# Prompt attention of a streaming encoder layer: the next pair's projection moved to steps 2 to 21, its norms across the edge, and a new slot table

## The chip, the cores and the metric

One core of a Trainium2 chip runs the whole layer in one launch. The metric is the device time of a run in microseconds; the median of three runs is compared.

## The reference, cut to what matters

The layer normalizes its input, projects it once (`w_in`), runs a recurrent branch and an attention branch, merges them and adds a mixture of experts. The change touches the attention branch alone, for a prompt of 1024 positions and for 64 new positions of a running stream with a cache of 2048:

```python
z = xn @ w_in
u_x, u_g, q, k, v, f_logit, g_rnn, g_attn = jnp.split(z, SPLIT_POINTS, axis=-1)
q = _rmsnorm(q.reshape(B, T, N_HEADS, HEAD_DIM), q_norm_g)
k = _rmsnorm(k.reshape(B, T, N_HEADS, HEAD_DIM), k_norm_g)
...
s = jnp.einsum('bqhd,bkhd->bhqk', q_blk, k).astype(jnp.float32) * scale
s = s + cq_blk.astype(jnp.float32).transpose(0, 2, 1)[..., None] - ckT
s = jnp.where(k_pos[None, :] <= q_pos[:, None], s, NEG_INF)
p = jax.nn.softmax(s, axis=-1)
return jnp.einsum('bhqk,bkhd->bqhd', p.astype(v.dtype), v)
```

There are 16 heads of 64. The normed k and the v are outputs too, for the prompt and for the stream.

## The kernel before

`attend` goes over 8 pairs of heads. The pairs 0 to 5 are turns of a loop, the pairs 6 and 7 are written out behind it. Pair i's attention is done in 24 steps, and while it runs, the q, k and v of pair i+1 are projected, normed and turned (`ahead`). Each engine runs its own program over the same steps; they meet in semaphores. Between pair i's step 23 and pair i+1's step 0 lies the edge of a pair.

**The steps.** `STEPS` lists four units (two heads, two halves of the queries) with their key tiles: unit 0 has steps 0 to 3, unit 1 steps 4 to 7, unit 2 steps 8 to 15, unit 3 steps 16 to 23. TensorE's program of a step s is: `score(s+1)` (L1125, L1127, and L1130 on the diagonal), then part 0 (a projection quarter, then the items of the slot), then `weigh(s)` (L1145), which needs ScalarE's `exp(s)` (L1344), then part 1 (a quarter, items). The tiles of scores and of probabilities have two buffers each.

**The projection.** A pair's 9 tiles of 128 positions have four quarters each, so 36 quarters, and a quarter is six products (`product`, L101 to L103) of 384 columns. Before, they go in pairs in the steps 0 to 17 (`PROJECT_STEPS`). There is one bank for them, `proj_ps`: behind the fourth quarter ScalarE copies it out and squares (`take_tile`), VectorE sums the squares (`sum_squares`), and only then may the next tile follow the copy. With tiles 0 to 3 done `mean 0` may run on VectorE, with tiles 4 to 8 `mean 1`; then ScalarE's `root` (L1295, a square root, behind which a small exponential L1385 brings the exponential's table back), then VectorE's `norm` 0 to 3 (L1463, L1464; tiles 0-1, 2-3, 4-5, 6-8), each of which raises `kv_ready`.

**The weights.** The projection's weights are in two parts, high and low. For pair i+2 they can be made only when pair i+1's projection has ended: SyncE loads w_in (L258) into one of two raw buffers, ScalarE rounds (`round_w`, L1289, items w 0 to 2), GpSimd subtracts (`rest_w`, L965). The columns of q (0) and v (2) share a raw buffer, so that the load of 2 waits for GpSimd's `rest_w` of 0, and `w 2` on ScalarE waits for that load.

**The items.** `SLOTS` says by hand which further work lies in which step and part. On each engine they are in the order of the table, and an engine waits where it stands:

- `max n`: a chunk of scores on TensorE (L1068, L1071) for the rows' maxima, one bank, reduced by VectorE (L1485). max 0 to 3 are for the next pair's unit 0, 4 to 7 for unit 1, and so on. `rows u` turns the maxima (L1059), ScalarE copies them (L1305), and `score` of the unit's first step waits for that.
- `qk0 b`, `qk1 b`: a head's q and k turned (L1053), copied by ScalarE (L1300, L1301) and by VectorE (`take_cross`, L1474). b is a batch of two tiles; b 0 and 1 are of the next pair, b 2 and 3 of this one. They wait for `kv_ready` of norm b.
- The stream: `qs`, `past n` (cached keys turned), `ss n` (scores of chunk n, L1204, L1205), their maximum (L1555) and exponential (L1378), `sp n` (turned, L1217, copied L1391), `sw n` (weighed, L1230, copied L1563). Chunk 4 is the short tail. Then `sum` (VectorE, L1569 to L1575) and `o` (turned, L1241). All items that turn share two banks, `turn_ps`, in strict alternation.
- `out u`: VectorE divides a unit's output (L1526, L1527). `out 3` comes behind step 23.

GpSimd also copies v (`take_v`), a part of the keys (`copy_high`, L972), and issues `load_c` (rows of the cumulated gates, L942; max 4 of the next pair waits for head 1's, `c_loaded`), `load_past_v` and `load_c_stream`. SyncE's queue holds the loads of weights and cached keys, the stores of k and v (L894 to L898) and of the attention's output (L907).

Of the kernel before, what the change touches and what calls it, by code (L numbers as in the profile page):

```python
# [775 lines left out]
def attend(nc, g):  # L776
# [10 lines left out]
    PROJECT_STEPS = 18  # L787
# [20 lines left out]
    FIRST_MAXES = 4  # L808
    NO_TURN = ("max", "out", "mean", "root", "norm", "w", "sum")
    later = lambda item: item[0] in ("mean", "root", "norm", "w") or item == ("rows", 0) or \  # L810
# [15 lines left out]
    with ExitStack() as ctx:  # L826
# [21 lines left out]
        warm = sb("warm", [P, 1])  # L848
# [15 lines left out]
        kv_ready, kv_stored, vs_copied = sem("kv_ready"), sem("kv_stored"), sem("vs_copied")  # L864
# [17 lines left out]
        with nc.Block() as block:  # L882
            @block.sync
            def _(sp):
# [7 lines left out]
                def store_kv(p):  # L892
                    sp.wait_ge(kv_ready, p * BATCHES + BATCHES)
                    sp.dma_start(heads(g.out_k_p[0, 0], p), qk_sb[:, 0:PT, 2:4, :].rearrange("p t h d -> p t (h d)")).then_inc(kv_stored, 16)  # L894
                    sp.dma_start(heads(g.out_v_p[0, 0], p), v_next[:, 0:PT, :]).then_inc(kv_stored, 16)
                    stream = lambda ap: ap.rearrange("t h d -> t (h d)")[:, bass.ds(p * P, P)]
                    sp.dma_start(stream(g.out_k_s[0, 0]), qk_sb[0:T_SAMPLE, PT, 2:4, :].rearrange("p h d -> p (h d)")).then_inc(kv_stored, 16)
                    sp.dma_start(stream(g.out_v_s[0, 0]), v_next[0:T_SAMPLE, PT, :]).then_inc(kv_stored, 16)  # L898
# [15 lines left out]
                store_kv(0)  # L914
                for done in g.early:
                    sp.sem_clear(done)
                with sp.Fori(0, PAIRS - 2) as i:
                    sp.wait_ge(w_split, i * 3 + 6)
                    alone(sp, g)
                    load_w(sp, g, i + 2, 0)  # L920
                    load_w(sp, g, i + 2, 1)
                    sp.wait_ge(w_split, i * 3 + 7)
                    alone(sp, g)
                    load_w(sp, g, i + 2, 2)
                    store_kv(i + 1)
                    probs_turned(i)
# [1392 lines left out]
```

## Time and profile before

| | |
|---|---|
| three runs | 2758.89, 2759.14, 2765.78 us; median 2759.14 |
| the profiled execution | 2751.23 us, of which the instructions span 2749.7 us |
| mean granted TensorE clock | 0.916 |
| TensorE, products | 2257.4 us busy (82%) |
| VectorE | 1328.1 us (48%) |
| ScalarE | 1116.7 us (41%) |
| GpSimd | 223.6 us (8%) |
| attention's pairs | from 185 to 1142 us |

Times in the trace are microseconds from the start of the span. "Idle before" is the time that an engine had nothing running ahead of an instruction, with what ended it. A granted clock of 1 is TensorE at 2.4 GHz, one of 0.5 at 1.2 GHz.

### The profile page before, as it was taken

To read this page: it belongs to the slowest core of one execution; us is meant where nothing else is said; L and a number is where in the kernel's file an instruction comes from. 1 tells how busy PE (TensorE), PEld (TensorE's weight loads), DVE (VectorE), ACT (ScalarE), POOL (GpSimd) and SP (SyncE) were. 2 spreads that over 40 slices of the span, in tenths; PEclk is the share of its full clock that TensorE was granted. 3 is DMA by queue.
4 is the path that set the end of the run, shared out by engine and by line. 5 is a ranking of instruction groups with operands and counts; after the bars stand their busy time and mean duration, and the time that the engine had idled before them with its cause. 6 is when DMAs were issued, how large, how long until landed. Compare 5 with 4: busy or idle time off the path is not lost. (4 is left out here: it accounts for less than half of the span.)

```text
span 2749.7 us, 36614 instructions
## 1 busy us (share of the span) xinstructions
PE 2257.4 (82%) x11080; PEld 1748.6 (64%) x11080; DVE 1328.1 (48%) x1548; ACT 1116.7 (41%) x1520; POOL 223.6 (8%) x294
## 2 busy tenths in 40 slices
PE   4459797887979797699899959989917999999991
PEld 2447565665757574499887849975415766666660
DVE  4334444445354444421155542111136888777884
ACT  3223343433333343221155632101105777777770
POOL 0210201202020200000012100000020000000002
PEclk9779898988989897899999979999958999999995
DMA  2210202112020202221156542133036999999986
GB/s 84 64 40 1 79 0 79 29 50 56 24 79 0 63 0 56 77 66 38 51 155 186 185 133 68 46 118 125 0 130 250 387 374 369 366 362 366 377 317 236
DMA packets 207115, 377.28 MB, mean 137 GB/s; under 512 B 20508, under 2 KB 128200, under 8 KB 206968
## 3 DMA queue, kind: packets, MB, share of 16 engines
q1 hardware_dynamic: 184680, 302.07, 32.2%
q0 software_dynamic: 18784, 61.92, 7.1%
q10 hardware_dynamic: 3584, 12.58, 1.2%
q8 instruction: 20, 0.33, 0.0%
q14 instruction: 47, 0.39, 0.0%
HBM read 301.87 MB, written 74.66 MB: 137 GB/s over the span
## 5 line engine op out<-in xcount | busy, mean ns | idle before, releaser
L2132 DVE TENSOR_TENSOR e_w_lo<-e_raw,e_w_hi 128x2048 fp32r<-128x2048 f32 x192 | 438.3, 2290 | 116.1 <-ACT e_w_hi L2059 107.2
L2059 ACT CAST e_w_hi<-e_raw 128x2048 fp32r<-128x2048 f32 x192 | 366.6, 1911 | 142.9 <-DMA e_raw<-w_down_e 60.0
L101 PE MATMUL proj_ps<-w_qkv_hi,xh 128*128 128x384 f32 x544 | 233.0, 428 | 21.6 <-PEq L286 19.2
L1145 PE MATMUL out_ps<-mT 128*128 128x512 f32 (+3 forms) x384 | 181.0, 556 | 23.2 <-ACT mT L1344 18.3
L103 PE MATMUL proj_ps<-w_qkv_hi,xl 128*128 128x384 f32 x544 | 187.9, 345 | 0.0
L102 PE MATMUL proj_ps<-w_qkv_lo,xh 128*128 128x384 f32 x544 | 187.3, 344 | 0.0
L1485 DVE TENSOR_REDUCE neg_part<-max_ps 128x1 f32<-128x512 f32 (+3 forms) x128 | 75.4, 589 | 133.0 <-PE max_ps L1071 72.7
L1344 ACT ACTIVATE mT<-st_ps 128x512 f32<-128x512 f32 x192 | 93.3, 489 | 109.1 <-PE st_ps L1130 48.3
L1671 PE MATMUL m_prod<-m_w_o,mT 128*128 128x512 f32 (+1 forms) x288 | 127.5, 602 | 11.2 <-DMA m_w_o<-w_o 11.2
L101 PEld LDWEIGHTS proj_ps<-w_qkv_hi,xh 128*128 128x128 f32 x544 | 107.2, 197 | 46.2 <-issue 40.7
L101 PE MATMUL e_gate_ps<-e_w_hi,e_xT_hi 128*96 128x512 f32 x256 | 105.8, 413 | 21.2 <-issue 10.5
L1474 DVE TENSOR_TENSOR qk_cross<-turn_ps,qk_high 64x256 fp32r<-64x256 f32 x128 | 53.4, 417 | 143.1 <-ACT qk_cross L1301 136.2
L102 PEld LDWEIGHTS proj_ps<-w_qkv_lo,xh 128*128 128x128 f32 x544 | 106.4, 196 | 20.6 <-issue 15.4
L1068 PE MATMUL max_ps<-qk_high 66*128 66x512 f32 (+1 forms) x192 | 82.0, 427 | 44.8 <-DVE extra L1485 33.4
L1125 PE MATMUL st_ps<-qk_high 67*128 67x512 f32 x192 | 89.5, 466 | 29.5 <-ACT qk_high L1305 18.0
L101 PE MATMUL e_y_ps<-e_w_hi,e_hT_hi 128*96 128x512 f32 x256 | 103.9, 406 | 11.1 <-DVE e_hT_lo L2140 9.1
L1526 DVE RECIPROCAL out_T<-out_ps 64x512 f32<-64x512 f32 x32 | 107.3, 3353 | 6.9 <-DVE o_part L1563 2.4
L1448 DVE TENSOR_REDUCE qk_rstd<-qk_squares 128x4 f32<-128x256 f32 x72 | 30.2, 420 | 160.3 <-ACT qk_squares L1284 157.9
L101 PE MATMUL e_up_ps<-e_w_hi,e_xT_hi 128*96 128x512 f32 x256 | 102.7, 401 | 4.1 <-issue 2.7
L103 PEld LDWEIGHTS proj_ps<-w_qkv_hi,xl 128*128 128x128 f32 x544 | 105.4, 194 | 0.0
L1671 PEld LDWEIGHTS m_prod<-m_w_o,mT 128*128 128x128 f32 (+1 forms) x288 | 53.4, 188 | 79.7 <-issue 68.2
L103 PE MATMUL e_gate_ps<-e_w_hi,e_xT_lo 128*96 128x512 f32 x256 | 102.8, 402 | 0.0
(402 smaller groups left out, 5330.3 us busy)
## 6 DMA issues: line engine op xcount, KB each, us to landing
e_raw<-w_gate_e SPq DMA_DIRECT2D x64, 1024.0 KB, 13.8
e_raw<-w_up_e SPq DMA_DIRECT2D x64, 1024.0 KB, 14.1
e_raw<-w_down_e SPq DMA_DIRECT2D x64, 1024.0 KB, 13.0
slot_x<-zrows POOLq DMA_DIRECT2D x48, 440.0 KB, 6.4
e_x<-slot_x SPq DMA_DIRECT2D x33, 384.0 KB, 11.3
w_raw<-w_in SPq DMA_DIRECT2D x24, 512.0 KB, 4.5
slot_y<-e_y ACTq DMA_DIRECT2D x32, 384.0 KB, 6.2
slot_y<-zrows POOLq DMA_DIRECT2D x24, 352.0 KB, 9.6
```

The lines of the kernel that those rows point to most:

```text
L101: nc.tensor.matmul(out, a_hi, b_hi, start=start, stop=False)
L102: nc.tensor.matmul(out, a_hi, b_lo, start=False, stop=False)
L103: return nc.tensor.matmul(out, a_lo, b_hi, start=False, stop=stop)
L1068: last = te.matmul(max_ps[:, 0:w], high[0:HD + 2, h, 0, t * P:(t + 1) * P], high[0:HD + 2, h, 1, c0:c0 + w], start=True, stop=not diagonal)
L1125: te.matmul(out[:, 0:q1 - q0], high[0:HD + 3, h, 1, j * P:(j + 1) * P], high[0:HD + 3, h, 0, q0:q1], start=True, stop=False)
L1145: te.matmul(out_ps[u % 2][:, q0 - c * BANK:BANK], v_one[:, j, h, :], probsT[s % 2][:, 0:q1 - q0], start=(j == 0), stop=(s == last_step(u)) ...
L1344: sc.activation(probsT[s % 2][:, 0:q1 - q0], st_ps[s % 2][:, 0:q1 - q0], ACT.Exp).then_inc(exp_ready, 1)
L1485: v.tensor_reduce(out, max_ps[:, 0:w], X_AXIS, ALU.max, negate=True).then_inc(max_taken, 1)
L1526: chain(v.reciprocal(into, out_ps[u % 2][other, n0:n1]))
L1671: last = te.matmul(prod[0:rows(t), t % 2, c * BANK:(c + 1) * BANK], g.mT[:, k, t * P:t * P + rows(t)], w_o[:, k, c * BANK:(c + 1) * BANK], ...
L2059: sc.copy(w_hi[u][:, :], w.raw[c][:, :]).then_inc(wh_ready, 1)
L2132: v.tensor_tensor(w_lo[u][:, :], w.raw[c][:, :], w_hi[u][:, :], ALU.subtract).then_inc(wl_ready, 1)
```

## The change

The quarters of the projection lie in the steps 2 to 17 in pairs and in the steps 18 to 21 one by one (36 as before). Norm 3 of a pair is done in step 1 of its own attention, norm 2 behind `o` in step 23; mean 1 goes to step 21, root 1 to 22, w 0 to 2 to 22 and 23, sum to 21. The stream's chunks have other slots: ss 0 in 5 instead of 7, ss 3 in 12 instead of 16, ss 4 in 14 instead of 18. qk0 3 goes from step 1 to step 2, behind rows 1. The stores of k and v go in two halves of 4 tiles. SyncE loads the cached keys ahead of the third weight load. GpSimd has another order. ScalarE begins each pair with a small exponential of its own.

```diff
-    PROJECT_STEPS = 18
+    PROJECT = {s: (1, 1) if s < 18 else (0, 1) for s in range(2, 22)}
+    LAST_NORM = 3
+    KV_STORES = (2, 4)
-    SLOTS = {0: ((), (("qk0", 2), ("max", 4))), 1: ((("max", 5),), (("qk0", 3), ("max", 6))),
-             2: ((("max", 7),), (("rows", 1), ("max", 8))), 3: ((("max", 9),), (("qs", 0), ("max", 10))),
-             4: ((("max", 11),), (("past", 0), ("max", 12))), 5: ((("max", 13),), (("past", 1), ("max", 14))),
-             6: ((("max", 15),), (("rows", 2), ("out", 0))), 7: ((("qk1", 2),), (("ss", 0), ("mean", 0))),
-             8: ((("qk1", 3),), (("sp", 0), ("max", 16))), 9: ((("max", 17), ("root", 0)), (("ss", 1),)),
-             10: ((("max", 18), ("sw", 0)), (("sp", 1),)), 11: ((("max", 19), ("past", 2)), (("sw", 1), ("norm", 0))),
-             12: ((("max", 20),), (("ss", 2), ("max", 21))),
-             13: ((("max", 22), ("sp", 2)), (("past", 3), ("max", 23), ("norm", 1))),
-             14: ((("rows", 3),), (("sw", 2), ("out", 1))), 15: ((), (("out", 2),)),
-             16: ((("qk0", 0),), (("ss", 3),)), 17: ((("qk0", 1),), (("sp", 3), ("mean", 1))),
-             18: ((("max", 0), ("w", 0)), (("sw", 3), ("ss", 4), ("root", 1))),
-             19: ((("max", 1), ("norm", 2)), (("sp", 4), ("w", 1))), 20: ((("max", 2), ("norm", 3)), (("sw", 4),)),
-             21: ((("max", 3),), (("w", 2),)), 22: ((("rows", 0),), (("qk1", 0), ("sum", 0))),
-             23: ((("qk1", 1),), (("o", 0),))}
+    SLOTS = {0: ((), (("qk0", 2), ("max", 4))), 1: ((("max", 5),), (("max", 6), ("norm", 3))),
+             2: ((("max", 7),), (("rows", 1), ("qk0", 3), ("max", 8))), 3: ((("max", 9),), (("qs", 0), ("max", 10))),
+             4: ((("max", 11),), (("past", 0), ("max", 12))), 5: ((("max", 13),), (("ss", 0), ("max", 14))),
+             6: ((("max", 15), ("sp", 0)), (("past", 1), ("rows", 2), ("out", 0))),
+             7: ((("qk1", 2), ("sw", 0)), (("ss", 1),)), 8: ((("qk1", 3),), (("sp", 1), ("max", 16))),
+             9: ((("max", 17),), (("sw", 1), ("past", 2), ("mean", 0))), 10: ((("max", 18), ("root", 0)), (("ss", 2),)),
+             11: ((("max", 19), ("sp", 2)), (("past", 3), ("norm", 0))),
+             12: ((("max", 20), ("sw", 2)), (("ss", 3), ("max", 21))),
+             13: ((("max", 22), ("sp", 3)), (("max", 23), ("norm", 1))), 14: ((("rows", 3),), (("ss", 4), ("out", 1))),
+             15: ((("sp", 4),), (("out", 2),)), 16: ((("qk0", 0),), ()), 17: ((("qk0", 1),), ()),
+             18: ((("max", 0),), ()), 19: ((("max", 1),), (("sw", 3),)),
+             20: ((("max", 2), ("sw", 4)), ()), 21: ((("max", 3),), (("mean", 1), ("sum", 0))),
+             22: ((("rows", 0), ("root", 1)), (("qk1", 0), ("w", 0))), 23: ((("qk1", 1), ("w", 1)), (("o", 0), ("norm", 2), ("w", 2)))}
...
+                def step(i, ahead, more):               # SyncE
+                    if more:
+                        sp.wait_ge(w_split, i * 3 + 6)
+                        alone(sp, g)
+                        load_w(sp, g, i + 2, 0)
+                        load_w(sp, g, i + 2, 1)
+                    store_kv(i, 1)
+                    if ahead:
+                        store_kv(i + 1, 0)
+                        probs_turned(i)
+                        load_past_k(i + 1)
+                    if more:
+                        sp.wait_ge(w_split, i * 3 + 7)
+                        alone(sp, g)
+                        load_w(sp, g, i + 2, 2)
+                    store_out(i)
...
                     copy_high(i + 1, 0, 0)              # GpSimd
+                    if more:
+                        rest_w(i + 2, 0)
                     weighed(last_step(3) - HALF)
                     take_v(i + 1, 1, 0)
-                    if more:
-                        rest_w(i + 2, 0)
-                        rest_w(i + 2, 1)
                     taken(NT)
                     take_v(i + 1, 0, 1)
+                    if more:
+                        rest_w(i + 2, 1)
+                        rest_w(i + 2, 2)
+                    pool.wait_ge(st_ready, i * NS + NS)
+                    alone(pool, g)
+                    load_c(i + 1, 1)
+                    copy_high(i + 1, 1, 0)
                     pool.wait_ge(sample_done, i * NP + NP)
                     alone(pool, g)
                     take_v_stream(i + 1)
                     load_past_v(i + 1)
                     load_c_stream(i + 1)
-                    if more:
-                        rest_w(i + 2, 2)
-                    pool.wait_ge(st_ready, i * NS + NS)
-                    alone(pool, g)
-                    load_c(i + 1, 1)
-                    copy_high(i + 1, 1, 0)
                     weighed(NS - 1)
...
                     x = 0                               # ScalarE
+                    sc.activation(warm[:, 2:3], g.ident[:, 0:1], ACT.Exp).then_inc(chain_a, 1)
                     exp(0)
...
-                for n in range(BATCHES):                # VectorE, ahead of the first pair
+                for n in range(LAST_NORM):
                     norm(chain, 0, n)
...
-                            norm(chain, i + 1, n)
+                            norm(chain, i + 1 if n < LAST_NORM else i, n)
```

## Rows read from the trace of the kernel before

**Rows 1.** The page: busy time, share of the span, instructions of each engine.

```profile
PE 2257.4 (82%) x11080; PEld 1748.6 (64%) x11080; DVE 1328.1 (48%) x1548; ACT 1116.7 (41%) x1520; POOL 223.6 (8%) x294
```

**Rows 2.** Windows inside pair 2: engines' busy us, then TensorE's clock, DMA share, GB/s.

```profile
444.70:516.10 71.40, 65.03 (x356) 51.70 (x356) 27.97 (x51) 26.85 (x63) 2.13 (x4) 1.00 0.00 0
...
527.80:539.00 11.20, 7.57 (x38) 4.29 (x35) 6.34 (x15) 8.86 (x19) 3.31 (x3) 1.00 0.07 18
539.00:555.60 16.60, 8.65 (x34) 5.51 (x32) 9.14 (x20) 4.50 (x9) 11.35 (x12) 0.60 0.79 206
555.60:567.70 12.10, 10.73 (x51) 8.55 (x52) 6.01 (x8) 3.94 (x8) 0.00 (x0) 0.84 0.52 149
```

**Rows 3.** Timeline, TensorE: scores 17, 18, 19 of pair 2; 0, 3 of pair 3.

```profile
516.15 0.39 PE L1125 MATMUL st_ps<-qk_high 67*128 67x512 f32 x1
...
522.12 0.50 PE L1125 MATMUL st_ps<-qk_high 67*128 67x512 f32 x1
...
527.78 0.48 PE L1125 MATMUL st_ps<-qk_high 67*128 67x512 f32 x1
...
555.59 0.76 PE L1125 MATMUL st_ps<-qk_high 67*128 67x512 f32 x1 [0.72 <-issue]
...
567.72 0.31 PE L1125 MATMUL st_ps<-qk_high 67*128 67x128 f32 x1
```

**Rows 4.** Waits, all pairs: waiting instruction, releaser, total us, times, longest.

```profile
PE turn_ps L1241 <- DVEq L84: 33.0, 8, 4.9
```

**Rows 5.** Timeline, TensorE: one quarter and what follows; one `ss` and what follows.

```profile
487.75 0.34 PE L101 MATMUL proj_ps<-w_qkv_hi,xh 128*128 128x384 f32 x1
...
488.80 0.39 PE L1068 MATMUL max_ps<-qk_high 66*128 66x512 f32 x1
```

**Rows 6.** The same view: a stream chunk's scores and the score behind them.

```profile
475.95 1.02 PE L1204 MATMUL turn_ps<-mT,q_s 128*128 128x512 f32 x2
...
477.32 0.50 PE L1125 MATMUL st_ps<-qk_high 67*128 67x512 f32 x1
```

**Rows 7.** Timeline, all engines, around the edge of pairs 2 and 3.

```profile
530.99 1.04 ACT L1289 CAST w_qkv_hi<-w_raw 128x1024 fp32r<-128x1024 f32 x1
...
533.77 1.28 ACT L1295 ACT_TABLE_LOAD   x1 [0.33 <-ACT mT L1378]
...
534.47 2.34 POOL L965 TENSOR_TENSOR w_qkv_lo<-w_raw,w_qkv_hi 128x1024 fp32r<-128x1024 f32 x1
...
535.30 1.28 ACT L1385 ACT_TABLE_LOAD   x1
...
537.04 0.37 SPq L258 DMA_DIRECT2D w_raw<-w_in  x1
...
539.98 3.00 DVE L1464 TENSOR_TENSOR qk_sb<-qk_sb,qk_gain 128x768 f32<-128x768 f32 x1
...
540.85 1.05 ACT L1289 CAST w_qkv_hi<-w_raw 128x1024 fp32r<-128x1024 f32 x1 [0.27 <-DMA w_raw<-w_in]
...
550.25 0.52 POOL L942 DMA_DIRECT2D qk_high<-c_rows  x1
...
556.30 3.35 DVE L1526 RECIPROCAL out_T<-out_ps 64x512 f32<-64x512 f32 x1 [0.26 <-DVE out_T L1580]
...
557.02 1.28 ACT L1344 ACT_TABLE_LOAD   x1 [6.01 <-PE st_ps L1130]
```

**Rows 8.** Landing of `load_c` (c_rows): windows 440 to 530 us, then 540 to 560.

```profile
DMA to landing us min/median/max: 2.0/2.0/2.0
...
DMA to landing us min/median/max: 6.3/6.3/6.3
```

**Rows 9.** Timeline: a norm of three tiles ahead of pair 0; the last pair's end.

```profile
162.92 0.96 DVE L1463 TENSOR_TENSOR qk_sb<-qk_sb,qk_rstd 128x768 f32<-128x768 f32 x1 [0.26 <-DVE qk_sb L1464]
...
1118.52 1.29 PE L1145 MATMUL out_ps<-mT 128*128 128x512 f32 x2 [4.07 <-DVEq L84]
...
1141.07 0.69 DVE L1527 TENSOR_TENSOR out_T<-out_ps,out_T 64x512 f32<-64x512 f32 x1
```

More of the change, by code:

```diff
@@ L808, in attend @@
     FIRST_MAXES = 4
     NO_TURN = ("max", "out", "mean", "root", "norm", "w", "sum")
-    later = lambda item: item[0] in ("mean", "root", "norm", "w") or item == ("rows", 0) or \
+    later = lambda item: item[0] in ("mean", "root", "w") or item == ("rows", 0) or (item[0] == "norm" and item[1] < LAST_NORM) or \
         (item[0] == "max" and item[1] < FIRST_MAXES) or (item[0] in ("qk0", "qk1") and item[1] < BATCHES // 2)
@@ L863, in attend @@
         c_loaded, cs_loaded, which_stored, which_loaded = [sem(f"c_loaded{h}") for h in range(2)], sem("cs_loaded"), sem("which_stored"), sem("which_loaded")
-        kv_ready, kv_stored, vs_copied = sem("kv_ready"), sem("kv_stored"), sem("vs_copied")
+        kv_ready, kv_stored, vs_copied = sem("kv_ready"), [sem(f"kv_stored{n}") for n in range(2)], sem("vs_copied")
         v_copied = [sem(f"v_copied{h}") for h in range(2)]
@@ L890, in load_past_k, with store_kv @@
                     sp.dma_start(k_past[:, :, :], heads(g.cache_k[0, 0], p)).then_inc(past_k_loaded, 16)
[L892 to L895, printed above, removed]
+                def store_kv(p, half):
+                    sp.wait_ge(kv_ready, p * BATCHES + 2 * half + 2)
+                    alone(sp, g)
+                    tiles = slice(half * HALF, (half + 1) * HALF)
+                    sp.dma_start(heads(g.out_k_p[0, 0], p)[:, tiles, :], qk_sb[:, tiles, 2:4, :].rearrange("p t h d -> p t (h d)"))\
+                        .then_inc(kv_stored[half], 16)
+                    sp.dma_start(heads(g.out_v_p[0, 0], p)[:, tiles, :], v_next[:, tiles, :]).then_inc(kv_stored[half], 16)
+                    if half == 0:
+                        return
                     stream = lambda ap: ap.rearrange("t h d -> t (h d)")[:, bass.ds(p * P, P)]
-                    sp.dma_start(stream(g.out_k_s[0, 0]), qk_sb[0:T_SAMPLE, PT, 2:4, :].rearrange("p h d -> p (h d)")).then_inc(kv_stored, 16)
-                    sp.dma_start(stream(g.out_v_s[0, 0]), v_next[0:T_SAMPLE, PT, :]).then_inc(kv_stored, 16)
+                    sp.dma_start(stream(g.out_k_s[0, 0]), qk_sb[0:T_SAMPLE, PT, 2:4, :].rearrange("p h d -> p (h d)")).then_inc(kv_stored[half], 16)
+                    sp.dma_start(stream(g.out_v_s[0, 0]), v_next[0:T_SAMPLE, PT, :]).then_inc(kv_stored[half], 16)
                 def probs_turned(i):
@@ L913, in _ @@
                 load_w(sp, g, 1, 2)
-                store_kv(0)
+                store_kv(0, 0)
                 for done in g.early:
                     sp.sem_clear(done)
-                with sp.Fori(0, PAIRS - 2) as i:
[L918 to L926, printed above, removed]
-                    load_past_k(i + 1)
-                    store_out(i)
-                store_kv(PAIRS - 1)
-                probs_turned(PAIRS - 2)
-                load_past_k(PAIRS - 1)
-                store_out(PAIRS - 2)
-                store_out(PAIRS - 1)
-                sp.wait_ge(kv_stored, PAIRS * 64)
+                def step(i, ahead, more):
[11 more added lines that the diff above has]
+                        sp.wait_ge(w_split, i * 3 + 7)
+                        alone(sp, g)
+                        load_w(sp, g, i + 2, 2)
+                    store_out(i)
+                with sp.Fori(0, PAIRS - 2) as i:
+                    step(i, True, True)
+                step(PAIRS - 2, True, False)
+                step(PAIRS - 1, False, False)
+                for half in range(2):
+                    sp.wait_ge(kv_stored[half], PAIRS * KV_STORES[half] * 16)
                 sp.wait_ge(pair_stored, PAIRS * 16 + 16)
@@ L985, in _ @@
                     rest_w(1, n)
-                pool.wait_ge(kv_ready, BATCHES)
+                pool.wait_ge(tile_taken, 2 * NT)
                 for half in range(2):
@@ L1247, in step @@
                             score(s + 1)
-                        counts = (1, 1) if ahead and s < PROJECT_STEPS else (0, 0)
+                        counts = PROJECT[s] if ahead and s in PROJECT else (0, 0)
                         for part in range(2):
@@ L1405, in step @@
                             exp(s + 1)
-                        counts = (1, 1) if ahead and s < PROJECT_STEPS else (0, 0)
+                        counts = PROJECT[s] if ahead and s in PROJECT else (0, 0)
                         for part in range(2):
@@ L1409, in step @@
                                 x += 1
[L1410 to L1411 removed]
+                                if x == 4 or x == 4 * HALF + 4:
+                                    half = x // (4 * HALF + 4)
+                                    act.wait_ge(kv_stored[half], i * (16 * KV_STORES[half]) + 16 * KV_STORES[half])
                                     alone(act, g)
[L1413 removed]
                                     for h in range(2):
[L1415 removed]
+                                        act.wait_ge(v_copied[h], i * 2 + half + 1)
                                         alone(act, g)
@@ L1584, in step @@
                     for s in range(NS):
-                        counts = (1, 1) if ahead and s < PROJECT_STEPS else (0, 0)
+                        counts = PROJECT[s] if ahead and s in PROJECT else (0, 0)
                         for part in range(2):
```

12 lines of the change are left out of this document (4 added, 8 removed).

## The prediction

> **What bounds the kernel now.** I began with the page for the engines' shares [rows 1]: TensorE is at 82%, no other engine above half. But the change touches only the attention of the prompt, 185 to 1142 us, so I went on to windows inside one pair [rows 2]. Of 71.4 us in the middle of a pair TensorE is busy for 65, at full clock. From 527.8 to 555.6 us, which are the steps 18 to 23 and the edge, it is busy for 16.2 us of 27.8, and in the second stretch its granted clock is 0.60, so that part of that busy time is work at 1.2 GHz. The middle of a pair is bound by TensorE, its edge by a chain over other engines. The reader is to see that a quarter of projection costs its full time in the middle and next to nothing at the edge.
>
> The timeline gives the yardstick: the scores' starts [rows 3]. From score 19 to score 0 of the next pair it takes 27.81 us, to score 3 (the beginning of step 2) 39.94 us, with four quarters in it, those of the steps 0 and 1. A quarter is 1.05 us, from its first product to what follows [rows 5]. The waits name one large stall: `o` waits for VectorE's sum, 33.0 us in 8 times [rows 4]. Around it the timeline shows the edge's pieces [rows 7]: the root with two table loads, 533.77 to 536.8; weights w 0 and w 2 with GpSimd and a load between, 530.99 to 541.9; a norm; the last `out`; and a table load of 1.28 us ahead of exp 0.
>
> **The change, part by part.** The sum is made against the profiled execution, 2751.2 us; the median of the runs lies 7.9 above it. TensorE's work stays the same.
>
> *Ahead of pair 0.* Norm 3 goes from VectorE's path to the first maxima: two passes of 0.96 us [rows 9], then max, rows, w 2, GpSimd and score 0 follow. I take 2 us. *Steps 0 and 1 of pair 0* lose four quarters (4.2 us). They are then a chain of maxima, not TensorE work; I take 4 us, for the table load [rows 7] goes off the path as well (ScalarE is idle 6 us there).
>
> *Steps 5 to 17.* The steps 5 to 15 get ss 3, sp 3, ss 4 and sp 4 in addition. An `ss` is 1.37 us [rows 6]; the others are transposes and short products, together 1.1 by their number of products. That is 2.5 us longer, less 0.5 of waiting for maxima that they fill. In four places an sp now stands closely behind its ss, whose maximum, exponential and semaphores take 2.2 us; I allow 1.0 us of waits in all (bounds: 0 and 4, one us each). The steps 16 and 17 last 11.6 us [rows 3]. They lose ss 3 and sp 3 (1.7 us) and a wait for the bank that ss 3 held behind `out 2`, and weigh 16 waits for `out 1` as before: by their work 3.4 and 4.1 us remain, so 4.1 gained. Net 4.1 - 2.0 - 1.0 = 1.1 a pair, seven pairs: 8.
>
> *The edge*, from score 19 = 0:
> - Steps 18 to 21: four scores, weighings and quarters (2.0 us a step), four maxima (0.9), sw 3 and sw 4 (1.2): 10.1 us.
> - Then no quarter is left. ScalarE's copies and square, the sum of squares and mean 1 take 2.8 us, root 1 with its two table loads 3.0, the copies of qk1 0 1.0. So w 0 begins at 17.2. The stall of [rows 4] goes, since sum ends near 15.6; late next is what follows w 0.
> - The weights' chain: w 0 1.04, GpSimd 2.34, load to landing and w 2's start 3.8, w 2 1.05 [rows 7], semaphores 0.5: w 2 ends at 25.8. Before, this ran beside `max`, `weigh` and the norms in steps 18 to 21; its cover is gone. Queued behind w 2 on ScalarE are the table load (1.28) and exp 0, so weigh 0 starts at 28.2, qk0 2 after it, max 4 could at 30.1.
> - Queued behind GpSimd's third subtraction (ends 28.4) is `load_c` of head 1, for which max 4 waits. It lands 2.0 us behind its issue when alone and 6.3 next to the cache's loads [rows 8]. These now stand behind it, but SyncE's store and two weight loads go off at that time. I take 3.5, nearer to the lone one: max 4 at 32.2. VectorE ends `o`, norm 2 and `out 3` (3.35 + 0.7, [rows 7, 9]) at about 28.3, so it isn't last.
> - Maxima 4, 5 and 6 go to and fro between TensorE and VectorE, 3.2 us: step 2 begins at 35.4, against 39.94. 4.5 gained, and as many quarters done.
> - Step 2 loses the wait behind qk0 3, step 3 gets it, norm 3 hides beside two quarters: 0.7 gained. The sparse stretch is all at 1.2 GHz, and work resumes so: before, 0.84 over 12.1 us [rows 2] is 3.9 us at the lower level, of which two were dense. I take 0.9 more.
>
> So 4.3 an edge, seven edges: 30. The edge of pairs 6 and 7 has no weights, but a VectorE chain of nearly that length.
>
> A norm of three tiles took 3.00 us in one pass beside GpSimd's subtraction, and 0.96 alone [rows 7, 9]. Norm 2 now lies next to the subtractions 1 and 2: one more pass of up to 2 us, and VectorE has some 2 us of slack there. In a sentence that the sum doesn't need: the Trainium skill, "SBUF — State Buffer", "Who interferes with whom", says that a VectorE instruction with two SBUF inputs and a GpSimd one that reads SBUF exclude each other, one with a single SBUF input doesn't. By it `take_cross` and `out 3`, which read PSUM, leave the subtractions alone; were it otherwise the chain would be some 1 us longer. The trace's 3.00 agrees.
>
> *The last pair.* Norm 3 comes in (1.9), and more sp stand close to their ss (4 us at most, I take 3). But from weigh 16 (1118.5) to the end (1141.8, [rows 9]) it is 23.3 us, with ss 3, sp 3, ss 4, sp 4 and the sum in it; eight steps of 1.4, `o` and `out 3` make 16. Net 2 to 3; 3 taken. The halved stores are bytes as before, on a queue with slack: 0 (bounds -1 and +2). The cached keys' load goes before the third weight load, 20 us earlier than its users need: 0.
>
> Sum: 2 + 4 + 8 + 30 + 3 = 47. 2751.2 - 47 = 2704; as a median 2759 - 47 = 2712.
>
> **The rivals.**
>
> *The weights' chain is longer than its pieces.* `load_c` lands in 6.3 (2.8 more), the load of w takes 5 instead of 3.7 beside other transfers (1.2), a subtraction is blocked once (0.7): 4.7 x 6 = 28 us back, 2740. For it: four engines in a row, and [rows 8]. Against it: the large loads are queued behind.
>
> *The clock profits.* The single quarters keep TensorE dense until step 21, and the low stretch of 16.6 us at 0.60 [rows 2], 13 us of which were at half clock, holds hardly any work: with 6 us of work at half clock before, 3 us x 7 = 21 more, 2691.
>
> *Slower: the clock stays down behind the edge.* The sparse stretch grows from about 16 us of mixed work to 22 us with almost none. Should TensorE then run its dense steps 2 onward at 1.2 GHz, each us of it costs half a us. It decides from (47 + 8)/7 = 8 us a pair, that is 16 us of dense steps at half clock; at 20 us the time is 2782. Against it: before, the clock was back about 2 us behind the first dense quarter. The Trainium skill, "TensorE: Matmul & The Clock Gate", section on a second failure mode, states that micro-idling between groups makes the clock go down and up, with a cost between bursts; by it the added idleness is such a cost, in this trace 2 us per edge.
>
> *The middle doesn't bear it.* The strict alternation of `turn_ps` stalls TensorE in steps 6 to 13 by 0.5 us a step: 28 us back, 2740.
>
> *The edge only swaps its stall.* `sum` is no longer waited for, but w 2 and `load_c` come as late as `o` did: the edge gains 0, 2742, with all other terms.
>
> **How the numbers follow.** The forecast, 2712, has 0.50 (own range 2698 to 2728). The weights' chain, the middle and the swapped stall, all near 2741, have 0.27 together, of which 0.06 lie within 0.3% (2751 and above). The clock's profit has 0.12. The slower clock 0.11, of which 0.09 beyond 2767. 0.3%, about 8 us, is what a measurement of this kernel can tell. The range goes from 2686, the profit with no waits, to 2750, the longest chain: 0.82 inside. Faster 0.83, within 0.08, slower 0.09.
>
> **What would show it.** After: score 19 to score 3 of the next pair near 36 us instead of 39.94; TensorE's wait at L1241 gone; ScalarE idle ahead of the last L1289 of a pair for some 5 us, ended by the DMA; TensorE's longest idle ahead of weigh 0 or max 4, released by the weights or by c_rows; steps 16 and 17 in 7.5 us instead of 11.6; steps 5 to 15 two to three us longer; a pair of about 118 us instead of 123.5. It would be wrong if low clock reached behind step 3, if TensorE waited for a bank in the middle, or if w 2 came later than 26 us behind score 19.

## The result

The changed kernel takes 2739.43 us in the median of five runs (2737.84 to 2748.19), the one before 2765.20 on the same occasion (2758.89 to 2771.35). The ratio is 0.9919, with a 95% interval of 0.9894 to 0.9944: faster, by some 22 us (15 to 29 by the interval). 2712, a gain of 47, had been forecast. The direction and the range (2686 to 2750) hold, the size is just under half.

The profiled execution took 2739.43 us, 11.8 less than that of before. The page of the kernel after, busy time by engine:

```profile
PE 2246.9 (82%) x11080; PEld 1745.7 (64%) x11080; DVE 1317.7 (48%) x1548; ACT 1122.6 (41%) x1528; POOL 219.4 (8%) x294
```

The shares of busy time tell nothing, as in [rows 1]. The scores' starts do. Timeline of the kernel after, TensorE: score 3, 16 and 19 of pair 2, then score 0 and 3 of pair 3:

```profile
439.83 0.46 PE L1137 MATMUL st_ps<-qk_high 67*128 67x128 f32 x1
...
512.03 0.48 PE L1137 MATMUL st_ps<-qk_high 67*128 67x512 f32 x1
...
523.33 0.39 PE L1137 MATMUL st_ps<-qk_high 67*128 67x512 f32 x1
...
544.49 0.77 PE L1137 MATMUL st_ps<-qk_high 67*128 67x512 f32 x1 [0.71 <-issue]
...
562.83 0.46 PE L1137 MATMUL st_ps<-qk_high 67*128 67x128 f32 x1
```

These three differences are the yardstick for all that follows, beside the attention stage's time from its first score to its last `out`:

| us | before | after | forecast |
|---|---|---|---|
| score 3 to 16 (steps 2 to 14) | 68.55 | 72.2 | 71.8 |
| score 16 to 19 (steps 15 to 17) | 14.49 | 11.30 | 10.4 |
| score 19 to score 3 of the next pair | 39.94 | 39.50 | 35.4 |
| sum, a pair inside the loop | 123.0 | 123.0 | 117.6 |
| attention stage | 956.9 | 946.6 | |

These are the figures of pair 2 and of its edge to pair 3, where no low clock falls into the middle. Such a pair takes as long as before: the whole middle and the whole edge have been rearranged for nothing. What the profiled execution gained lies at the ends and in a few pairs. The first score comes 2.6 us sooner (184.84 to 182.27). From it to score 3 it is 10.4 us instead of 13.2. The pairs 3 and 4 had a low clock in their middle before (126.7 and 125.2 us instead of 123.0), together 6.0. The edge of pairs 5 and 6 is 3.7 shorter (36.56 against 40.27), that of 6 and 7 0.9 (32.48 against 33.43), while the middles of these two pairs are 0.6 longer together. The last pair, from its score 3, is 2.0 us longer; the loop's first two pairs are 0.5 longer. That makes 12.9, and 1.1 are lost behind attention. All seven edges together went from 274.9 to 266.6 us, 8.3 less. A second profiled execution of the kernel before gave 956.9 us for the stage again, the pairs 3 and 4 with a low clock again. Everything outside the stage, where no line is changed, took between 1764 and 1808 us in these fourteen profiles. So the 22 us of the ratio hold some 10 that no stretch of attention shows; I can't assign them.

The edge after, in windows: steps 18 to 21, the rest up to weigh 0, weigh 0 to score 3, steps 2 and on (busy by engine, clock, DMA share, GB/s). To be held against [rows 2]:

```profile
523.30:535.20 11.90, 11.90 (x63) 9.08 (x62) 3.92 (x11) 2.92 (x7) 0.15 (x1) 1.00 0.00 1
535.20:554.60 19.40, 5.89 (x32) 3.65 (x30) 12.53 (x22) 11.97 (x20) 9.53 (x9) 0.68 0.10 29
554.60:562.80 8.20, 6.07 (x17) 3.47 (x18) 1.55 (x4) 1.33 (x3) 3.55 (x6) 0.50 0.92 253
562.80:574.80 12.00, 10.41 (x56) 8.43 (x56) 4.89 (x8) 2.43 (x6) 0.61 (x1) 0.87 0.40 101
```

TensorE is solidly busy in the steps 18 to 21, as forecast, and then has 5.9 us of work in 19.4. The idle time that used to be spread has been collected. TensorE's clock is at 0.50 from score 0 to score 3, where it was back at 1.00 from weigh 0 on before. The chain through it, timeline of all engines, where [rows 7] stood before:

```profile
538.05 1.28 ACT L1307 ACT_TABLE_LOAD   x1 [0.61 <-DVEq L84]
...
539.59 1.28 ACT L1397 ACT_TABLE_LOAD   x1
...
542.10 1.04 ACT L1301 CAST w_qkv_hi<-w_raw 128x1024 fp32r<-128x1024 f32 x1
...
543.33 2.36 POOL L977 TENSOR_TENSOR w_qkv_lo<-w_raw,w_qkv_hi 128x1024 fp32r<-128x1024 f32 x1 [19.88 <-ACT w_qkv_hi L1301]
543.38 0.39 PE L1253 MATMUL turn_ps<-ident,o_s 128*64 128x128 f32 x1 [4.67 <-DVEq L1558]
...
545.93 0.39 SPq L258 DMA_DIRECT2D w_raw<-w_in  x1
...
546.98 2.71 DVE L1477 TENSOR_TENSOR qk_sb<-qk_sb,qk_gain 128x512 f32<-128x512 f32 x1
...
549.67 1.04 ACT L1301 CAST w_qkv_hi<-w_raw 128x1024 fp32r<-128x1024 f32 x1 [4.58 <-DMA w_raw<-w_in]
...
552.19 1.28 ACT L1414 ACT_TABLE_LOAD   x1 [1.48 <-issue]
...
554.67 2.05 PE L1157 MATMUL out_ps<-mT 128*128 128x512 f32 x2 [7.97 <-ACT mT L1356]
...
557.22 0.46 PE L1080 MATMUL max_ps<-qk_high 66*128 66x128 f32 x1
...
558.80 0.87 DVE L1487 TENSOR_TENSOR qk_cross<-turn_ps,qk_high 64x256 fp32r<-64x256 f32 x2 [4.78 <-ACT qk_cross L1313]
560.10 0.29 DVE L1498 TENSOR_REDUCE extra<-max_ps 128x1 f32<-128x128 f32 x1 [0.43 <-DVE qk_cross L1487]
```

It is read from the brackets: ScalarE waits 4.58 us for the load behind w 0 and GpSimd, TensorE 7.97 us for ScalarE's exp 0, GpSimd 19.88 us for w 0. The wait ahead of `o` [rows 4] is still there, 32.9 us in 7 times, but its releaser is another: no longer the sum but the bank that qk1 0 holds (L1558 releases it behind `take_cross`), which is late since ScalarE's root is in front of qk1 0.

### The profile page after: what moved, and what is told of

It reads as the page before. It is cut to its first block and busy times, and to the rows that moved or that the text cites. A ratio compares the mean times of both kernels' runs of the same rounds, so it can differ in the third digit from the quotient of the medians.

```text
span 2737.9 us, 36710 instructions
## 1 busy us (share of the span) xinstructions
PE 2246.9 (82%) x11080; PEld 1745.7 (64%) x11080; DVE 1317.7 (48%) x1548; ACT 1122.6 (41%) x1528; POOL 219.4 (8%) x294
## 3 DMA queue, kind: packets, MB, share of 16 engines
q1 hardware_dynamic: 184936, 302.07, 32.5%
## 5 line engine op out<-in xcount | busy, mean ns | idle before, releaser
L1137 PE MATMUL st_ps<-qk_high 67*128 67x512 f32 x192 | 85.4, 445 | 27.1 <-ACT qk_high L1317 11.9
## 6 DMA issues: line engine op xcount, KB each, us to landing
e_raw<-w_down_e SPq DMA_DIRECT2D x64, 1024.0 KB, 13.2
```

Of the source, the lines that this page charges most:

```text
L1137: te.matmul(out[:, 0:q1 - q0], high[0:HD + 3, h, 1, j * P:(j + 1) * P], high[0:HD + 3, h, 0, q0:q1], start=True, stop=False)
```

## The experiments

Between executions, the parts outside attention move by more than most edits do, so I give the stage's time and its stretches, from one profiled execution each, and the ratio to the kernel before with its interval. Ratios of two rows are hard to compare: e11, whose stage is the changed kernel's within 0.7 us, has 0.9873 against 0.9919.

| | 3 to 16 | 16 to 19 | 19 to 3 | stage | ratio |
|---|---|---|---|---|---|
| before, twice | 68.55 | 14.49 | 40.2, 40.5 | 956.9 | |
| after | 72.2 | 11.30 | 39.5 | 946.6 | 0.9919 (0.9894 to 0.9944) |
| e2 max 4 first | 71.3 | 11.30 | 38.1 | 936.4 | 0.9896 (0.9838 to 0.9954) |
| e3 chunks back | 68.4 to 70.3 | 14.49 | 40.4 | 952.9 | 0.9953 (0.9910 to 0.9995) |
| e4 w 2 in the next pair | 72.2 | 11.30 | 35.6 | 928.0 | 0.9852 (0.9791 to 0.9913) |
| e5 e2 and e4 | 72.2 | 11.29 | 34.3 | 918.5 | 0.9851 (0.9787 to 0.9916) |
| e6 before, sum early | 69.8 | 14.50 | 41.6 | 960.3 | 1.0016 (0.9966 to 1.0065) |
| e7 norms alone | 69.4 | 14.51 | 37.4 | 941.1 | 0.9943 (0.9900 to 0.9986) |
| e8 norms, sum early | 69.4 | 14.50 | 34.2 | 924.8 | 0.9893 (0.9812 to 0.9975) |
| e9 TensorE kept busy | 72.3 | 11.29 | 38.5 | 946.1 | 0.9944 (0.9891 to 0.9996) |
| e10 e8, max 4 first | 69.4 | 14.49 | 32.5 | 913.6 | 0.9814 (0.9774 to 0.9854) |
| e11 load_c sooner | 72.2 | 11.29 | 39.4 | 945.9 | 0.9873 (0.9799 to 0.9948) |
| e12 e6, late cache loads | 68.5 | 14.49 | 36.6 | 931.5 | 0.9880 (0.9822 to 0.9939) |

The stretches are those of the pairs inside the loop (19 to 3: the mean of the first five edges, for e12 the usual one; 3 to 16: the usual one, in e6 with some low clock in it and 68.5 without).

**e2, e4, e5: what stands in the edge's chain.** e2 exchanges two items:

```diff
-    SLOTS = {0: ((), (("qk0", 2), ("max", 4))),
+    SLOTS = {0: ((), (("max", 4), ("qk0", 2))),
```

> The changed kernel with the slot of step 0 in the other order: max 4 ahead of qk0 2. Theory (the edge is one serial chain: last quarter, square and mean, root, w 0, GpSimd, load, w 2, exp 0, weigh 0, then qk0 2, take_cross, max 4, 5, 6 in turn): VectorE's max 4 no longer stands behind take_cross, max 5's reduction can start some 1.1 us sooner, and score 3 follows score 19 after 38.4 us instead of 39.5; 8 us less over the attention. Rival (the clock at 1.2 GHz sets the edge's length): the products between weigh 0 and step 2 take as long as before, below 0.3 us an edge. Rival (load_c of head 1 holds max 4): max 4 would wait longer, no gain.

38.1 us, 1.4 less than the changed kernel: the theory, a little more. The stretch from weigh 0 to score 3 falls from 8.2 to 6.5 us, but its clock rises too, from 0.50 to between 0.65 and 0.75, so this run alone doesn't part the two. e5 against e4, below, does.

e4 takes w 2 off the last step (and off the stretch ahead of pair 0):

```diff
-    SLOTS = {0: ((), (("qk0", 2), ("max", 4))),
+    SLOTS = {0: ((), (("qk0", 2), ("max", 4), ("w", 2))),
...
-             22: ((("rows", 0), ("root", 1)), (("qk1", 0), ("w", 0))), 23: ((("qk1", 1), ("w", 1)), (("o", 0), ("norm", 2), ("w", 2)))}
+             22: ((("rows", 0), ("root", 1)), (("qk1", 0), ("w", 0))), 23: ((("qk1", 1), ("w", 1)), (("o", 0), ("norm", 2)))}
...
+                        elif what == "w" and n == 2:
+                            round_w(i + 1, n)
...
-                        rest_w(i + 2, 2)
...
                     take_v(i + 1, 1, 1)
+                    if more:
+                        rest_w(i + 2, 2)
```

> The changed kernel with w 2 taken off the end of step 23 and put behind qk0 2 and max 4 in step 0 of the next pair, and GpSimd's third subtraction behind load_c. Theory (exp 0 stands behind w 2, which waits for a load): ScalarE no longer waits 4.6 us there; weigh 0 comes some 5 us sooner, and then VectorE's out 3, which ends about 30.7 us behind score 19, is last: score 3 follows score 19 after some 35 us instead of 39.5; about 27 us less over six edges and 1 us ahead of the first pair. Rival (the mean and the root set the edge, the weights are hidden): below 1 us an edge. Rival (load_c is last): the same gain as the theory's or less than 1 us, and TensorE's long wait moves to L1080 (max 4).

35.56 us at every edge of the loop, 928.0 us for the stage. The timeline of e4 shows who is last now: ScalarE goes straight from w 1 to its table load, weigh 0 waits 0.79 us, and the next long wait is TensorE's for VectorE, which has norm 2 and `out 3` in front of take_cross and max 4:

```profile
532.60 1.28 ACT L1418 ACT_TABLE_LOAD   x1
...
535.03 2.05 PE L1160 MATMUL out_ps<-mT 128*128 128x512 f32 x2 [0.79 <-ACT mT L1358]
...
537.46 3.35 DVE L1543 RECIPROCAL out_T<-out_ps 64x512 f32<-64x512 f32 x1 [0.26 <-DVE qk_sb L1481]
...
538.99 0.45 PE L1083 MATMUL max_ps<-qk_high 66*128 66x128 f32 x1 [0.55 <-DMA qk_high<-c_rows]
...
544.12 0.55 PE L1083 MATMUL max_ps<-qk_high 66*128 66x256 f32 x1 [3.88 <-DVE extra L1502]
```

> The two edits of e2 and e4 together. Theory: behind out 3 VectorE takes max 4 at once; score 3 follows score 19 after about 34 us; some 33 us less than the changed kernel. If the clock set the edge, no more than 5 us less.

34.3 us, 918.5 for the stage, 28 less than the changed kernel. So the new chain over the weights is worth 3.9 us an edge and the order in step 0 another 1.3; from weigh 0 to score 3 it is 10.1 us instead of e4's 11.4, at a clock of 0.50 in both. Whole executions don't show the step from e4 to e5 (0.9852 and 0.9851). A third raw buffer, with which all three weight loads could go at once, was not tried.

**e11: is `load_c` in it?**

```diff
                         rest_w(i + 2, 1)
-                        rest_w(i + 2, 2)
                     pool.wait_ge(st_ready, i * NS + NS)
                     alone(pool, g)
                     load_c(i + 1, 1)
+                    if more:
+                        rest_w(i + 2, 2)
```

> The changed kernel with GpSimd's load_c and its wait ahead of the third subtraction. Theory: load_c landed 2.0 us ahead of where max 4 stood, so it holds nobody: score 3 follows score 19 after 39.5 us as before, within 0.5. Rival (load_c is on the path): 1.5 us less or more.

39.4 us: inside the loop of the changed kernel it holds nobody. There it landed 2.1 us after 553.17, ahead of max 4 at 557.22. It stands next in the row, though: max 4 waits 0.55 us for `c_rows` in e4, 1.9 us in e5, and 0.96 us at the changed kernel's own edge of pairs 5 and 6.

**e9: is the clock what ate the gain?** Ahead of weigh 0 TensorE does work for nobody:

```diff
+                            if part == 0 and s == 0 and ahead:
+                                pe.wait_ge(tile_taken, 2 * ((i + 1) * NT))
+                                alone(pe, g)
+                                for _ in range(24):
+                                    te.matmul(proj_ps[:, 0:QKV], g.xh[:, 0, 0:P], g.xh[:, 0, 0:QKV], start=True, stop=True)
                             if part == 0:
                                 weigh(s)
```

> The changed kernel with 24 products of 384 columns that nobody reads, ahead of weigh 0 of pairs 0 to 6, where TensorE waits 8 us for exp 0 anyway; they write the projection's bank, which is free then. Theory (the edge is a chain over ScalarE, GpSimd, a load and VectorE): the clock comes back sooner, and the products of the steps 0 and 1 get shorter, but score 3 follows score 19 after 38.5 us or more instead of 39.5. Rival (the low clock is what ate the gain): 36.5 us or less.

Windows of e9: up to weigh 0, weigh 0 to score 3:

```profile
535.00:555.00 20.00, 11.71 (x60) 9.35 (x58) 12.77 (x23) 11.52 (x20) 9.16 (x7) 0.83 0.10 27
555.00:563.00 8.00, 5.40 (x19) 3.12 (x19) 1.55 (x4) 1.78 (x5) 3.95 (x8) 0.76 0.88 254
```

TensorE's clock averages 0.76 between weigh 0 and score 3 instead of 0.50, and the edge is 1.0 us shorter (38.5, between 37.8 and 38.9); the stage is not (946.1), because in pair 0 the added work is in nobody's shadow (14.0 us from score 0 to score 3 instead of 10.4). That much of the clock gives back 1 us an edge. What the full clock would give there no run shows. An estimate of its most: TensorE is busy for 6.1 us of that stretch at half clock, so 3 us, less than the 4 that are missing.

**e3: what moving the stream's chunks is worth.** All past, ss, sp and sw items are back where they were, the rest as changed (ss 0 in step 7, ss 3 in 16, ss 4 in 18, and so on).

> The changed kernel with the stream's items (past, ss, sp, sw) back in the steps where they were; projection, norms, stores, weights and sum as changed. Theory (work moved out of steps 16 to 19 into the dense middle is moved at its full price): score 3 to score 16 falls from 72.2 to 68.8 us, score 16 to 19 rises from 11.3 to 14.3, the edge stays at 39.5 or rises by 1 us (VectorE later); within 5 us of the changed kernel in all. Rival (the sooner chunks lengthen the middle without giving it back): 20 us faster than the changed kernel. Rival (the sooner chunks are what makes the change faster): 15 us slower, the last pair above all.

Timeline of e3, TensorE: score 3, 16, 19 of pair 2:

```profile
440.32 0.46 PE L1136 MATMUL st_ps<-qk_high 67*128 67x128 f32 x1
...
509.92 0.51 PE L1136 MATMUL st_ps<-qk_high 67*128 67x512 f32 x1
...
524.41 0.48 PE L1136 MATMUL st_ps<-qk_high 67*128 67x512 f32 x1
```

The steps 15 to 17 take their 14.49 us again, the steps 2 to 14 some 3 us less (3.8 where no low clock falls into them; in pair 2, shown, one did). The exchange is at full price: inside the loop it gains and loses the same. The edge is 0.9 longer and the stage 6.3. So the sooner chunks are neutral to slightly good, 1 us more than the 5 that were expected at most, and not what made the change good.

**e7, e8, e10: the norms without the projection.** The changed code, with its halved stores and its order on GpSimd and SyncE, but with the projection in steps 0 to 17 and mean 1, root 1, w and the stream where they were before:

```diff
-    PROJECT = {s: (1, 1) if s < 18 else (0, 1) for s in range(2, 22)}
+    PROJECT = {s: (1, 1) for s in range(18)}
...
+             16: ((("qk0", 0),), (("ss", 3),)), 17: ((("qk0", 1),), (("sp", 3), ("mean", 1))),
+             18: ((("max", 0), ("w", 0)), (("sw", 3), ("ss", 4), ("root", 1))),
+             19: ((("max", 1),), (("sp", 4), ("w", 1))), 20: ((("max", 2),), (("sw", 4),)),
+             21: ((("max", 3),), (("w", 2),)), 22: ((("rows", 0),), (("qk1", 0), ("sum", 0))),
+             23: ((("qk1", 1),), (("o", 0), ("norm", 2)))}
```

e8 has the sum a step sooner as well (step 21: w 2, then sum 0), e10 that and max 4 ahead of qk0 2.

> The norms and the halved stores alone: norm 2 behind o, norm 3 and qk0 3 as in the changed kernel, GpSimd's and SyncE's order too; the projection in steps 0 to 17, the stream's chunks, mean 1, root 1, w and sum where they were before. Theory (the weights' chain is long hidden in steps 18 to 21, and norms 2 and 3 hold up max 2 and 3 there): score 3 follows score 19 after some 37 us instead of 39.9, 18 us less than the kernel before, so faster than the whole change. Rival (the norms only come back at the edge): 39 to 41 us.

> e7 with the sum in step 21 as well. Theory: both waits gone and the weights still hidden, score 3 follows score 19 after 34.5 us with four quarters in it; some 35 us less than the kernel before and 25 less than the changed one. Rival (the move of the quarters is what gains, the rest nothing): as the kernel before.

> e8 (norms and halved stores, sum in step 21, projection in steps 0 to 17, chunks and weights where they were) with max 4 ahead of qk0 2 in step 0. Theory: as in e2, 1.2 us less an edge than e8; the attention lasts some 916 us from the first score to the last out, against 957 before, 946 in the changed kernel and 925 in e8. Rival (with quarters in steps 0 and 1 VectorE's order hides behind them): as e8.

e7: 36.0 to 38.4 us, 941.1 for the stage, so without the moved projection the stage is 5.5 us shorter than with the whole change (946.6). Whole executions don't show that (0.9943 against 0.9919, overlapping intervals). e8: 32.9 to 35.8 us, 924.8. e10: 32.0 to 34.2, 913.6, the best of all, with a median of 2703.64 us against 2753.67 for the kernel before. The weights are then made in steps 18 to 21, beside max, weigh and scores, and nobody waits for them.

These runs don't part the norms from the order of the loads, which comes with the changed code: the cached keys' load is issued 6.5 us behind score 19 in e8 (19.5 before) and the cached values' 1.0 us behind ScalarE's last instruction of the pair, so that the DMA engines are idle in ScalarE's 1.14 us of "issue" there. e12, below, leaves the norms where they were and gets 25.4 of e8's 32.1 us. And the length of an edge follows the clock: in e7 the edges of 38.1 to 38.4 us and those of 36.0 to 36.2 take turns, with a mean clock of 0.78 and 0.86.

e10 came out at the time that had been expected, but for the most part not by the order of step 0: its edges gain mainly between score 0 and weigh 0, where nothing was exchanged. Windows of that stretch of pair 3, e8 and then e10:

```profile
536.67:540.70 4.03, 4.03 (x12) 3.21 (x13) 3.13 (x5) 2.28 (x4) 3.26 (x6) 0.50 0.61 160
```

```profile
531.46:533.76 2.30, 2.30 (x12) 1.63 (x13) 1.66 (x4) 2.22 (x4) 2.30 (x4) 1.00 0.29 52
```

The same work runs at 1.00 instead of 0.50. Why the clock stays up there no run shows. Timeline of e10, TensorE: score 19 of pair 2, score 0 and 3 of pair 3:

```profile
509.66 0.48 PE L1138 MATMUL st_ps<-qk_high 67*128 67x512 f32 x1
...
531.46 0.47 PE L1138 MATMUL st_ps<-qk_high 67*128 67x512 f32 x1 [0.84 <-issue]
...
541.77 0.31 PE L1138 MATMUL st_ps<-qk_high 67*128 67x128 f32 x1
```

**e6 and e12: the sum alone, and what stood behind it.** In the kernel before:

```diff
-             21: ((("max", 3),), (("w", 2),)), 22: ((("rows", 0),), (("qk1", 0), ("sum", 0))),
+             21: ((("max", 3),), (("w", 2), ("sum", 0))), 22: ((("rows", 0),), (("qk1", 0),)),
```

> The kernel BEFORE with one item moved: sum from step 22, behind qk1 0, to step 21, behind max 3. Theory (in the kernel before the edge's last wait is VectorE's sum, and nothing else stands close behind it): o goes when qk1 0's bank is free, at 551.3 instead of 554.5 us of the trace; score 3 follows score 19 after 36.7 us instead of 39.9; 20 us less over the attention. Rival (the edge swaps the stall, as it did in the changed kernel): below 1 us an edge.

Neither the theory nor its rival: 41.6 us, 1.3 more than the mean before, and 1.8 more at the edge of pairs 2 and 3, of which the following lines are. `o` and score 0 do come 2.7 us sooner, 25.1 us behind score 19 instead of 27.8. But exp 0 is not sooner by as much, and weigh 0 starts 31.3 us behind score 19 instead of 31.8. Timeline of e6, ScalarE from its last instruction of pair 2, and TensorE's weigh 0; then what the DMA engines did from the one to the other:

```profile
556.29 0.36 ACT L1301 CAST qk_cross<-turn_ps 64x256 fp32r<-64x256 f32 x1
...
562.40 1.28 ACT L1344 ACT_TABLE_LOAD   x1 [5.74 <-issue]
...
564.74 2.05 PE L1145 MATMUL out_ps<-mT 128*128 128x512 f32 x2 [2.90 <-ACT mT L1344]
```

```profile
DMA packets 2330, 1.41 MB, mean 248 GB/s; under 512 B 199, under 2 KB 2247, under 8 KB 2325
...
q1 hardware_dynamic: 2078, 1.05, 74.2%
q0 software_dynamic: 251, 0.35, 22.9%
q14 instruction: 1, 0.01, 0.5%
```

The rest of the loss lies behind weigh 0. Windows from there to score 3, e6 and then the kernel before:

```profile
564.74:575.20 10.46, 9.34 (x40) 7.26 (x40) 1.55 (x4) 1.71 (x5) 0.00 (x0) 0.75 0.53 154
```

```profile
559.57:567.72 8.15, 6.78 (x41) 5.45 (x40) 2.33 (x6) 1.70 (x5) 0.00 (x0) 1.00 0.68 197
```

The same work takes 2.3 us more at a clock of 0.75 instead of 1.00, behind TensorE's wait of 2.90 us for exp 0. That is why this edge is 1.8 us longer and not 0.5 shorter.

5.74 us of "issue": ScalarE waited for no semaphore that the trace shows. It is the turn of the loop, and among 2330 packets there is one of the kind "instruction". Before, the same time can have been there unseen: ScalarE's 6.01 us [rows 7] were put down to the score, which ended at 556.9 us, 5.9 behind ScalarE's last instruction. The Trainium skill, "Runtime: NRT & Kernel Launch", section "Instruction fetch mechanics", says that a taken branch whose target isn't in the current window of two pages of instructions forces a DMA fetch before execution goes on. That ScalarE's turn is such a fetch and stands behind the data of the two loads was the new theory, and e12 tests it by issuing the two loads of 1 MB later:

```diff
                     store_kv(i + 1)
+                    store_out(i)
                     probs_turned(i)
                     load_past_k(i + 1)
-                    store_out(i)
...
                     take_v_stream(i + 1)
-                    load_past_v(i + 1)
...
-                    for h in range(2):
-                        copy_high(i + 1, h, 1)
+                    copy_high(i + 1, 0, 1)
+                    load_past_v(i + 1)
+                    copy_high(i + 1, 1, 1)
```

> e6 (the kernel before with the sum early) with the two loads of cached keys and values, 1 MB each, issued later: the keys behind the attention's output store, the values behind qk0 3 of step 1. Theory (in e6 ScalarE stood 5.7 us at the loop's turn with nothing to wait for but its own next instructions, whose fetch lay behind those loads): the idle time ahead of its table load falls to 1.5 to 3 us, and score 3 follows score 19 after 37 to 38.5 us instead of 41.6. Rival (the turn takes ScalarE its time whatever the DMA queues do): 5 us or more of idle again, 41 us or more.

Timeline of e12, TensorE's scores 19 and 3 and between them ScalarE over the same turn; then its DMA from 545.5 to 548 us:

```profile
522.25 0.48 PE L1125 MATMUL st_ps<-qk_high 67*128 67x512 f32 x1
...
545.16 0.36 ACT L1301 CAST qk_cross<-turn_ps 64x256 fp32r<-64x256 f32 x1
...
547.89 1.28 ACT L1344 ACT_TABLE_LOAD   x1 [2.37 <-PE st_ps L1130]
...
558.93 0.30 PE L1125 MATMUL st_ps<-qk_high 67*128 67x128 f32 x1
```

```profile
DMA packets 2, 0.02 MB, mean 7 GB/s; under 512 B 0, under 2 KB 0, under 8 KB 0
...
q14 instruction: 2, 0.02, 1.6%
```

The turn is no longer what ScalarE waits for: its 2.37 us end with the score, and the only packets are instructions. What the chip fetches in them, and for which engine, the trace doesn't name. That the wait is the fetch is therefore not shown, and the changed kernel speaks against taking every turn so: in its 1.48 us of "issue" (550.71 to 552.19) the DMA view has no packet at all. That the loads' place decides is shown. The edge is 36.6 us, the stage 931.5, 25.4 less than before and 28.8 less than e6; the ratios, 0.9880 and 1.0016, have intervals that don't meet. Of the 5 us an edge between e6 and e12, 3.2 lie ahead of weigh 0 (28.1 us behind score 19 instead of 31.3) and 1.9 behind it, at a clock of 0.95 instead of 0.75. That the same sum, moved by one step, costs 3 us with the loads in front of the turn and gains 25 without is the clearest thing that these runs show, though e6's 3 us can't be told from nothing by its ratio. What the late loads alone would give, without the sooner sum, was not run.

**The kernel before again.**

> The kernel before once more, for one look. Theory: within attention every stretch repeats to some tenths of a us but for low clock in the middle of a pair, so 953 to 958 us from the first score to the last out; what lies outside attention differs between executions by 10 us and more.

956.9 us, the same to a tenth; outside attention 1787.5 instead of 1792.8.

## Why the prediction was right or wrong

*The sign held, and so did several terms.* Ahead of pair 0: 2 forecast, 2.6 measured. Steps 2 to 15: 3.2 us longer forecast, 3.8 measured. norm 2 beside a subtraction: 2.71 us in its second pass, as the prediction allowed. The chain's core was right to some tenths: the last quarter to w 0, 6.9 us (7.1 forecast), w 0 to the end of w 2, 8.61 (8.6). Pair 0's opening gave less, 2.8 instead of 4, and so did steps 16 and 17, from score 17 to 19: 8.3 us where 7.5 had been forecast (11.6 before). With that a middle without low clock loses 0.5 us where 0.9 had been forecast as gained, some 9 us over seven pairs.

*The term that failed is the edge: 4.3 us each and 30 in all forecast, 0.4 measured from pair 2 to 3 and 8.3 over all seven.* The forecast had score 3 at 35.4 us behind score 19; it came at 39.5. From score 19 it goes: steps 18 to 21 took 11.9 us instead of 10.1, so a step of score, weigh and quarter comes to 2.4 and not 2.0, if maxima and sw cost what had been forecast. The chain from there was 0.2 shorter, so that w 2 ended 1.6 late. Between w 2's end and weigh 0 lay 4.0 us instead of 2.4: the loop's turn, 1.48 us on ScalarE, was in no row that I had costed. From weigh 0 to max 4, 2.6 instead of 1.9. `load_c` was allowed 2.1 us and took none (e11). And from max 4's start to score 3 it was 5.6 us instead of 3.2: I had costed the maxima to and fro between two engines, but not that VectorE takes `take_cross` of qk0 2 first, which waits for ScalarE's copies. e5 against e4 shows that order's price at one clock, 1.3 us. Together 1.6 + 1.6 + 0.6 - 2.1 + 2.4: 4.1.

*The low clock in the edge* had no term of its own. It was 0.50 from score 0 to score 3, where TensorE had been back at 1.00 from weigh 0 on before. By how much it makes the 5.6 us long is open: e9 got 1.0 back with part of the clock, and e11's edges, which take turns, need 8.15 us from weigh 0 to score 3 at 0.50 and 7.3 at 0.72. The 0.9 that had been forecast was for the steps behind the edge. There the clock is at 0.87 over 12 us, which is 3.1 us at the lower level and costs at most 1.6, part of the 3.8 above.

*The order of the rivals.* The fifth, that the edge only swaps its stall, is what came: the sum's wait left, the weights' wait came, and e4 takes it away again. It named `load_c` too, which held nobody. It had been given 0.27 together with two others. That its 2742 is near the measured 2739 is partly luck, for it kept all other terms, of which the middle and the last pair gave less, and the kernel before ran 6 us above the median that it started from. The idle time that the quarters filled in the steps 18 to 21 was time in which the weights were being made. That this cover would go was in the prediction; that the chain without it is as long as what it replaced was not.

*One exception fits.* At the edge of pairs 5 and 6 ScalarE leaves its loop, so that the turn isn't taken (TensorE's and VectorE's loops go on to pair 6). Timeline of the kernel after, ScalarE at that edge:

```profile
918.43 1.04 ACT L1301 CAST w_qkv_hi<-w_raw 128x1024 fp32r<-128x1024 f32 x1 [4.58 <-DMA w_raw<-w_in]
919.38 0.20 ACT L1414 ACTIVATE warm<-ident 128x1 f32<-128x1 f32 x1
```

The 1.48 us of "issue" and the table load of 1.28 us are both gone, and weigh 0 starts 28.4 us behind score 19 instead of 31.3; score 3 comes 2.9 us sooner as well. e3, e9 and e11, with the weights in the way too, have that edge 2.7 to 3.4 us shorter than the others, e4 and e5, without them, don't have it shorter. e2 has it only 0.3 shorter, since max 4 then waits 1.81 us for `c_rows`.

*The last pair* was forecast 3 shorter and is 2.0 longer: its steps 2 to 14 rose from 53.8 to 61.2 us, of which 4 or 5 had been allowed. 5.2 of these 7.4 us are more time with TensorE busy (42.4 to 47.6), 2.2 more idle time, such as 1.6 us ahead of an ss for a bank. A wait ahead of an sp, which had been allowed for, shows in one place, with 1.05 us. Behind score 16 it gained 5.3 where 7.3 had been forecast from weigh 16 on.

*What stays open*: some 10 us of the ratio's gain, outside attention or in executions that weren't profiled; and what makes the low clock end where it does, in the edges and, in the kernel before, in the middle of pairs 3 and 4, twice out of twice.

## What to carry to other kernels

Idle time of the main engine is often somebody's cover. Before work is moved into it, list what the other engines do in it, and ask what that will stand beside afterwards. Here the change without the moved projection, with the sum early, gave 32 us in the stage (e8), with max 4 first 43 (e10), instead of 10. The move itself does little harm once the weights are off the path: e5, with the quarters moved, gave 38.

In an edge of several chains of nearly equal length a change to one gains only down to the next. Cost each up to a common end, in the order in which each engine meets its items, and price the loop's turn as an item on each.

## What the runs showed of the hardware

ScalarE's turn of the loop took 5.74 us with large loads under way (e6, 248 GB/s), 1.0 to 1.5 us without (after, e7, e8, e10), and in e4 the table load began 0.01 us behind w 1. It shows as idle time put down to "issue", ahead of the first instruction of the next turn. Issuing two loads of 1 MB behind the turn instead of ahead of it was worth 28.8 us of the stage (e6 against e12). An estimate from pair 2's edge, 1.9 us times five, puts some 10 of it down to the higher clock behind weigh 0.

24 products ahead of weigh 0 brought TensorE's clock from 0.50 to 0.76 of full over the following 8 us, and the edge got shorter by 1.0 us only. The kernel's own work moves it as well: from score 0 to weigh 0 TensorE took 4.03 us at 0.50 (e8) and 2.30 at 1.00 (e10).
